# Attention scores of a two-block transformer on one core: only 512 key columns a head in the dilated layer, and latent-attention heads on halves and quarters of the rows

## What is computed

```python
A_PATTERNS = ((128, 1), (512, 4), (2048, 16))      # window, dilation
def dilated_band_attention(q, k, v, window, dilation):
    """Centred dilated window: query t attends t + j*dilation, |j| <= window/(2*dilation)."""
...
    wts = jax.nn.softmax(lses, axis=0)
    return jnp.einsum('pbsh,pbshc->bshc', wts.astype(q.dtype), outs)
```

```python
    q_c = jnp.concatenate([q_nope, q_rope], axis=-1)[:, :, :, None]
    k_c = jnp.concatenate([k_nope, jnp.broadcast_to(k_rope[:, :, None], (b, s, C_HEADS, C_ROPE))], axis=-1)
    c_out = block_attention(q_c, k_c, v_c)
```

## Time and profile before

| | us |
|---|---|
| median of 3 runs | 4381.66 |
| lowest, highest | 4380.32, 4391.59 |
| the profiled execution | 4382.55 |
| its span on the core | 4380.8 |

### The profile page before, as it was taken

How to read it: one execution, slowest core, us unless ns; L and a number is a source line. 1 busy time by engine, 2 the same in 40 slices (tenths; PEclk the granted TensorE clock), 3 DMA queues, 4 the chain that set the end, 5 groups by cost and what they waited for, 6 DMA issues and landing times. The chain is left out here.

```text
span 4380.8 us, 56560 instructions
## 1 busy us (share of the span) xinstructions
PE 3830.7 (87%) x22320; PEld 3130.2 (71%) x22320; DVE 2545.0 (58%) x3879; ACT 1673.6 (38%) x2291; POOL 334.7 (8%) x207
## 2 busy tenths in 40 slices
PE   6988999988989999998898999499678898994996
PEld 2666778767777888887796877277577786872774
DVE  6256772159765566556334763677654566735775
ACT  2223332146330000003114763267534565732775
POOL 0001111000000000000000000033100000000441
PEclk9989999989999999999999999699889999996998
DMA  7101123230432111112213004299723203032997
GB/s 288 59 23 56 58 73 97 82 132 20 154 135 82 38 57 38 57 39 86 89 58 143 31 16 151 87 370 364 247 65 105 53 21 114 14 137 80 367 376 277
DMA packets 178217, 518.88 MB, mean 118 GB/s; under 512 B 20000, under 2 KB 113344, under 8 KB 159952
## 3 DMA queue, kind: packets, MB, share of 16 engines
q1 hardware_dynamic: 158384, 454.42, 28.6%
q0 software_dynamic: 16496, 59.36, 4.6%
q10 hardware_dynamic: 3120, 2.10, 0.2%
HBM read 427.21 MB, written 88.62 MB: 118 GB/s over the span
## 5 line engine op out<-in xcount | busy, mean ns | idle before, releaser
L2077 ACT ACTIVATE mlp_relu<-mlp_z 128x512 f32<-128x512 f32 x64 | 38.3, 598 | 616.0 <-PE mlp_z L157 616.0
L3174 DVE TENSOR_TENSOR ring_r<-ring,oN_r 128x4096 fp32r<-128x4096 f32 x48 | 212.1, 4423 | 70.0 <-ACT oN_r L3105 69.9
L155 PE MATMUL scans_G<-ring_r 128*128 128x512 f32 x544 | 221.7, 408 | 32.3 <-ACT scans_stg L2624 18.3
L3174 DVE TENSOR_TENSOR ring_r<-ring,hT_r 128x4096 fp32r<-128x4096 f32 x48 | 212.4, 4424 | 55.4 <-ACT hT_r L3105 55.3
L3105 ACT ACTIVATE oN_r<-ring 128x4096 fp32r<-128x4096 f32 x48 | 174.0, 3630 | 86.7 <-DMA ring<-in_w_all 73.4
L155 PE MATMUL mlp_z<-oN_r,mlp_w_high_r 128*128 128x512 f32 x512 | 200.2, 391 | 5.6 <-DVE ring_r L2118 5.6
L3105 ACT ACTIVATE hT_r<-ring 128x4096 fp32r<-128x4096 f32 x48 | 174.0, 3630 | 68.2 <-DMA ring<-in_w_all 68.0
L156 PE MATMUL mlp_z<-hT_r,mlp_w_high_r 128*128 128x512 f32 x512 | 199.9, 390 | 0.0
L157 PE MATMUL mlp_z<-oN_r,ring_r 128*128 128x512 f32 x512 | 199.9, 390 | 0.0
L155 PE MATMUL mlp_y_ps<-mlp_w_high_r,ring_r 128*128 128x512 f32 x512 | 199.6, 390 | 0.0
L157 PE MATMUL mlp_y_ps<-mlp_w_high_r,ring_r 128*128 128x512 f32 x512 | 199.2, 389 | 0.0
(11 more groups left out here) (644 smaller groups left out, 10515.0 us busy)
## 6 DMA issues: line engine op xcount, KB each, us to landing
ring<-in_w_all SPq DMA_DIRECT2D x118, 2048.0 KB, 10.6
ring<-in_w_mlp SPq DMA_DIRECT2D x16, 2048.0 KB, 7.7
ring<-in_w_all SPq DMA_DIRECT2D x12, 1024.0 KB, 6.3
branch_gates<-scans_stg SPq DMA_DIRECT2D x48, 256.0 KB, 2.0
merge_raw<-branch_gates SPq DMA_DIRECT2D x16, 768.0 KB, 5.1
ring<-in_w_even SPq DMA_DIRECT2D x4, 1536.0 KB, 6.7
qk_turned<-even_gemm_y SPq DMA_DIRECT2D x48, 128.0 KB, 1.9
even_qk<-qk_turned SPq DMA_DIRECT2D x6, 1024.0 KB, 4.9
```

The costliest lines, as they stand in the source:

```text
L155: pe.matmul(out, lh, rh, start=start, stop=False)
L2077: act.activation(r[:, n % 2, :], Z[:, n % 4, :], ACT.Relu).then_inc(z_free, 1)
L3174: dve.tensor_tensor(buf_r[:, b, :], buf[:, b, :], w_high[n % RING].bitcast(F32), ALU.subtract)\
```

## The change

**Even attention** gets a stage of its own, `even_stage`. A block scores 512 columns a head in place of 1024: 256 keys around the block (its 128 tokens and 64 on either side) in three passes on F32R, and for each of the four classes modulo 4 the 32 queries of the class against the 256 keys of that class, as eight plain float32 matmuls (4 classes by 2 heads; 64 rows, 32 stationary columns, 256 moving columns read with a step of 4 elements), each writing 32 partitions. For this the queries of a block are kept in the order of their classes. The shift, the exponential, the transposes (8 a block) and the copies into `pT` halve. The values are made with `pT` stationary: for each head 2 matmuls with the near values (128 stationary, 64 moving columns) and 8 with the class values (32 stationary, 64 moving columns). The result is scaled on DVE (`norm`), turned once on PE (`turn_out`) and copied by ACT into `hT` in token order (`take_out`). q, k and their high parts lie in two ring slots, so this stage feeds two weight slots, and the other two are fed by the out_even stage behind its x loads. The values come in five DMAs a pair in place of one (1.2 MB in place of 0.5), and the table in eight.

**Latent attention**: the 64 position-free components of the two heads go on rows 0 to 63 and 64 to 127, as in even and gqa. The rotary 32 come as a second set: for each pass four matmuls on rows 0, 32, 64 and 96 onwards (2 heads by 2 halves of the keys), added to the same banks. `mla_gemm` writes ten tiles of 128 rows and one of 32, by 5 transposes a step (6 in every other), two ACT copies where three were, no copy of the shared part, one DMA a step and a small second one in every other. `w_mla` is laid out for this by twelve DMAs in place of one.

```diff
-            sp.dma_start(w_mla.rearrange("p (h n) -> p h n", h=8), m["w_mla"].rearrange("h p n -> p h n")).then_inc(mla_in, 16)
+            for g in range(2):
+                heads = m["w_mla"][4 * g:4 * g + 4, :, :].rearrange("h p n -> p h n")
+                for to, of, n in ((0, 0, 64), (256, 64, 32), (384, 96, 64), (640, 160, 32), (768, 192, 64), (1024, 256, 64)):
+                    at = g * (MLA_W // 2) + to
+                    sp.dma_start(w_mla[:, at:at + 4 * n].rearrange("p (h n) -> p h n", h=4), heads[:, :, of:of + n])                      .then_inc(mla_in, 16)
...
-                    for j in range(2 * G):
-                        ins = pe.transpose(TP[0:W, i % 2, j, :], x[:, i % 3, j * W:(j + 1) * W], m["ident"][:])
-                    ins.then_inc(xt_done, 1)
+                    if i % 2 == 0:
+                        pe.transpose(TP[0:RO, 0, NB, :], keep_rope[:, i // 2, :], m["ident"][:])
+                    for j in range(2):
+                        pe.transpose(TP[:, i % 2, j, :], x[:, i % 3, j * P:(j + 1) * P], m["ident"][:])
+                        pe.transpose(TP[:, i % 2, 2 + j, :], x[:, i % 3, KN + j * P:KN + (j + 1) * P], m["ident"][:])
+                    pe.transpose(TP[:, i % 2, 4, :], x[:, i % 3, 2 * P:KN], m["ident"][:]).then_inc(xt_done, 1)
...
-                        sp.dma_start(qk[:, b, :, a, :], m["qkT"][8 * a + 2 * p:8 * a + 2 * p + 2, 0:96, :]
-                                     .rearrange("h p n -> p h n")).then_inc(qk_in[b], 16)
+                        sp.dma_start(qk[:, b, a * S:(a + 1) * S], m["qkT"][5 * g + 2 * a + j, :, :]).then_inc(qk_in[b], 16)
+                    for hd in range(2):
+                        for half in range(2):
+                            r = 64 * hd + 32 * half
+                            sp.dma_start(qk[r:r + 32, b, QR], m["qkT"][5 * g + 4, 64 * j + 32 * hd:64 * j + 32 * hd + 32, :])\
+                              .then_inc(qk_in[b], 16)
+                            if p == 0:
+                                sp.dma_start(qk[r:r + 32, 0, KR], m["qkT"][10, 0:32, half * HALF:(half + 1) * HALF])\
...
-                        for hd in range(2):
-                            for half in range(2):
-                                cols = slice(half * HALF, (half + 1) * HALF)
-                                ins = three_passes(pe, SA[:, 2 * hd + half, :],
-                                                   [q_[:, b, hd, 0, toks] for q_ in (qk_high, qk_low)],
-                                                   [k_[:, b, hd, 1, cols] for k_ in (qk_high, qk_low)], True, True)
-                            ins.then_inc(scored, 1)
+                        (qh, kh), (ql, kl) = ((t_[:, b, 0:S][:, toks], t_[:, b, S:2 * S]) for t_ in (qk_high, qk_low))
...
+                    passes = ((qh, kh), (qh, kl), (ql, kh))
+                    for half in range(2):
+                        cols = slice(half * HALF, (half + 1) * HALF)
+                        for j, (q_, k_) in enumerate(passes):
+                            for hd in range(2):
+                                r = slice(64 * hd, 64 * hd + 64)
+                                ins = pe.matmul(SA[:, 2 * hd + half, :], q_[r, :], k_[r, cols], start=j == 0,
+                                                stop=j == 2 and not mla)
+                                if half == 1 and j == 2 and not mla:
+                                    ins.then_inc(scored, 1)
+                    if mla:
+                        (qh, kh), (ql, kl) = ((t_[:, b, QR][:, toks], t_[:, 0, KR]) for t_ in (qk_high, qk_low))
+                        for j, (q_, k_) in enumerate(((qh, kh), (qh, kl), (ql, kh))):
+                            for hd in range(2):
+                                for half in range(2):
+                                    r = slice(64 * hd + 32 * half, 64 * hd + 32 * half + 32)
+                                    ins = pe.matmul(SA[:, 2 * hd + half, :], q_[r, :], k_[r, :], start=False, stop=j == 2)
+                                if j == 2:
+                                    ins.then_inc(scored, 1)
...
+def even_stage(nc, m):
+
+
+    with Stage(nc, "even") as st:
+        PAIRS, NEAR, CLS = 6, 2 * P, 4
+        N, SUB, WIN = PAIRS * NT, P // CLS, 384
+        LEN = S // CLS
+        SCALE = 0.125
+        spare = [(m["ring"].used + 2 + j) % RING for j in range(2)]
...
+                b = p % 2
+                if p >= 2:
+                    sp.wait_ge(scored, 2 * NT * (p - 1))
+                sp.dma_start(raw[:, b, :, :], m["qkT"][2 * p:2 * p + 2, :, :].rearrange("a p n -> p a n")).then_inc(qk_in[b], 16)
+                if p == 0:
+                    rows = m["dilated"].rearrange("(i r) n -> r i n", r=CLS)
+                    for r in range(CLS):
+                        sp.dma_start(table[SUB * r:SUB * r + SUB, 0:WIN], rows[r, :, 896 - P:896 - P + WIN]).then_inc(near_in, 16)
+                    for r in range(CLS):
+                        sp.dma_start(wide_table[SUB * r:SUB * r + SUB, :], rows[0, :, :]).then_inc(wide_in, 16)
+                if p >= 2:
+                    sp.wait_ge(pv_done, NT * (p - 1))
+                v = m["v"][:, P * p:P * p + P]
+                for tiles, first in ((slice(0, 7), 64), (slice(7, 9), 0), (slice(9, 11), S - NEAR)):
+                    count = (tiles.stop - tiles.start) * P
+                    sp.dma_start(v_near[:, b, tiles, :], v[first:first + count, :].rearrange("(t p) c -> p t c", p=P))\
+                      .then_inc(v_in[b], 16)
+                for half in range(2):
...
+            def scores(n):
+                p, qb = divmod(n, NT)
+                b, toks = p % 2, slice(qb * P, (qb + 1) * P)
+                if qb == 0:
+                    pe.wait_ge(low, 2 * (p + 1))
+                if n >= 2:
+                    pe.wait_ge(shifted, 2 * (n - 1))
+                for r in range(CLS):
+                    for hd in range(2):
+                        d = slice(64 * hd, 64 * hd + 64)
+                        pe.matmul(SA[SUB * r:SUB * r + SUB, 2 * (n % 2) + hd, NEAR:HALF], raw[d, b, 0, toks][:, r::CLS],
+                                  raw[d, b, 1, r::CLS], start=True, stop=True)
+                keys = slice(first_key(qb), first_key(qb) + NEAR)
+                (qh, kh), (ql, kl) = ((t_[:, b, 0, toks], t_[:, b, 1, keys]) for t_ in (qk_high, qk_low))
+                for j, (q_, k_) in enumerate(((qh, kh), (qh, kl), (ql, kh))):
+                    for hd in range(2):
+                        d = slice(64 * hd, 64 * hd + 64)
+                        ins = pe.matmul(SA[:, 2 * (n % 2) + hd, 0:NEAR], q_[d, :], k_[d, :], start=j == 0, stop=j == 2)
+                        if j == 2:
...
+            def turn(u):
...
+                for k in range(4):
...
+            def values(w):
+                p, qb = divmod(w, NT)
+                b = p % 2
+                if qb == 0:
+                    pe.wait_ge(v_in[b], 16 * 5 * (p // 2 + 1))
+                if w >= 2:
+                    pe.wait_ge(taken, w - 1)
+                for hd in range(2):
+                    pe.wait_ge((ev_act, ev_dve)[hd], w + 1)
+                    pt, c = pT[:, (2 * w + hd) % 4, :, :], slice(64 * hd, 64 * hd + 64)
+                    for k, t in enumerate(near_tiles(qb)):
+                        pe.matmul(O[:, w % 2, c], pt[:, k, :], v_near[:, b, t, c], start=k == 0, stop=False)
+                    for half in range(2):
+                        for r in range(CLS):
+                            i = slice(SUB * r, SUB * r + SUB)
+                            ins = pe.matmul(O[i, w % 2, c], pt[:, 2 + half, i], v_class[:, b, half, r, c], start=False,
...
+            def turn_out(w):
+                pe.wait_ge(normed, w + 1)
+                pe.transpose(OT[:, w % 2, :], o[:, w % 2, :], m["ident"][:]).then_inc(o_turned, 1)
+
+            for n in range(-1, N + 2):
+                if n + 1 < N:
+                    scores(n + 1)
+                if 0 <= n < N:
+                    turn(2 * n)
+                if n >= 2:
+                    turn_out(n - 2)
+                if 1 <= n <= N:
+                    values(n - 1)
+                if 0 <= n < N:
+                    turn(2 * n + 1)
+
...
+                act.activation(m["hT"][:, p, qb * P:(qb + 1) * P].rearrange("p (i r) -> p r i", r=CLS),
+                               OT[:, w % 2, :].rearrange("p (r i) -> p r i", r=CLS), ACT.Copy).then_inc(taken, 1)
+
...
+                    dve.wait_ge(t_done, u - 3)
+                dve.memset(wait_taker[:, u % 4:u % 4 + 1], 0.0)
+                dve.tensor_tensor_reduce(out=sc[:, u % 4, :].rearrange("p (w c) -> p w c", w=2),
+                                         in0=SA[:, u % 4, :].rearrange("p (w c) -> p w c", w=2),
+                                         in1=times_of(u // 2 % NT), scale=-SCALE, scalar=-LOWEST, op0=ALU.add, op1=ALU.min,
+                                         accum_out=nm[:, u % 8:u % 8 + 1]).then_inc(shifted, 1)
...
```

(10 more changed lines are left out.)

234 lines of the change are left out of this document (172 added, 62 removed).

## The result

The changed kernel takes 4316.0 us (4 runs, 4308.2 to 4318.9), the kernel before, run beside it, 4383.7. The ratio is **0.984, with a 95% interval of 0.982 to 0.985**: 65 to 77 us gained. 4327 had been predicted, in a range of 4288 to 4372.

A forecast was written before the change was run, and what follows sets the result against it. PE was taken to bound both attentions. Gains of 39.8 us (even blocks), 3, 5, 5.1, 2.4 and 1, less 1.5 lost, sum to 54.8: from 4382.55 to 4327.7, 4327 as a median, range 4288 to 4372.

The forecast's parts named there:

- Even block: Even attention, one block on PE: parts sum to 4.81 us against 5.64, 39.8 us gained in 48 blocks.
- class scores: Even block on PE: eight two-pass matmuls, all eight side by side at about 0.06 each, 0.50 us.
- class values: Even block on PE: 16 matmuls at 0.06 each, 0.96 us.
- seven changes: Even block on PE: seven changes of tile shape at 0.16 each, 1.12 us.
- the stepped read: Rival, even class scores: reading keys with a 16-byte step halves the stream; 0.95 us, 21.6 us more, 4349; chance 0.13.
- 16 x 0.06, the issue rate again: Even class values: 16 matmuls priced by how fast matmuls can be issued, 0.96 us; small transposes started some 0.07 apart.
- all side by side: Rival, even and mla blocks: no issue bound; class values 0.3, rotary 0.69, even block 4.1 to 4.2; 4295 us; chance 0.14.
- The two slow rivals: Even and mla blocks: only two tiles work side by side, 4424 us, chance 0.10; or each matmul costs 0.109, 4402, 0.08.
- Pair changes: Even stage: DVE's low part and ACT's casts no longer fit in one block; 0.3 for each of five, 1.5 us lost.
- Start: Even stage's first loads and cast: smaller loads ahead, and two half casts let DVE start before ACT ends; 3 us gained.
- mla_gemm, 5 predicted: mla_gemm's 16 steps: both sides of the balance shorten by about 0.3 us a step, 5 us gained, ends 3 and 6.
- Latent attention, 6.50 predicted: mla block on PE: 6.50 us against 6.66, rotary part 0.72 by issue; 5.1 us gained, pair changes 2.4 more.

The follow-up runs named there:

- the two experiments: Changed kernel with, per mla_gemm step, one more 128-column copy on DVE (2.55 us a step) or two more transposes on PE (2.57), against 2.41.
- class_order: Changed kernel with even_gemm writing q and k with each 128 tokens sorted by class: 4289.2 us, 0.977 of the kernel before.

## Why the prediction was right, and where its terms were not

The mechanism was right: PE bounds both attentions before and after, and small tiles run side by side. The forecast was 11 us too high, and inside it larger errors stood against each other. By the stretches 17 us more were gained than the sum has, and stages outside the change hide 8 of them in the span. So that the time came out this close is in part luck.

- **Even block, 4.81 predicted, 4.62 measured.** Term by term, with 0.14 for a change of shape (predicted, then measured):

| term | predicted | measured |
|---|---|---|
| class scores | 0.50 | 0.93 (1.07 less a change) |
| near scores | 0.37 | 0.35 (three of 0.117) |
| transposes, turn_out | 0.98 | 0.98 |
| near values | 0.88 | 0.89 |
| class values | 0.96 | 0.45 (0.36 less a change, twice) |
| seven changes | 1.12 | 1.0 (what is left of 4.62) |

  Two terms failed, in opposite directions. (The near scores' 0.37 was a slip: three times half of 0.23 is 0.35.) *Class scores*: the stepped read, which the prediction held as a rival with 0.95 and a chance of 0.13, is real. *Class values*: the step "16 x 0.06, the issue rate again" was wrong. It took the 0.07 of four small transposes as a bound on how fast matmuls can be issued; passes start 7 ns apart here, and sixteen take 0.22 us. The rival that priced this about rightly (all side by side, 0.3) gave 4295 since it had no stepped read beside it. The two rivals were treated as exclusive; both came true, and that they cancelled to 0.08 us is luck.
- **The Trainium skill on tiles** (TensorE: Matmul & The Clock Gate, Part 3) was followed only halfway in the prediction, which kept its own bound from a row against "starts about 4 ns apart". The trace agrees with the page's rule: in the rotary part four F32R matmuls start 3 to 4 ns apart, as the page has it. Passes on plain float32 start 6 to 7 ns apart.
- **The Trainium skill on the step** (SBUF — State Buffer, Specifications: 16-byte cachelines, with a penalty for each cross to a new line) is borne out in the direction. It names no size. Here a pass of 256 keys goes from 0.24 to 0.44 us when the keys step by 16 bytes in place of lying in runs of 32 (queries in a row in both), and from 0.27 to 0.47 against keys in one row (queries stepped in both).
- **The two slow rivals** (two tiles at a time, 0.109 a matmul) are out by the same rows: eight tiles start within 0.047 us.
- **Pair changes, 1.5 us lost predicted, 2.1 gained.** "Before, it fitted" was wrong: the kernel before has a block of 6.06 in place of 5.64 at each of five pair changes, which one block of the earlier trace rows didn't show. In the changed kernel the casts (3.1 us) and DVE's low part (3.3) are even longer than assumed, and are hidden all the same. They begin to show in blocks of 4.33 and cost 0.4 us a pair change at 4.15 and 0.8 at 3.85; of the 0.8 the larger part stands behind ACT's cast.
- **Start, 3 predicted, 0.5 measured, and a term that was missing, 6.2.** The two half casts are not equal. ACT and DVE, with q first and k behind it, where the earlier trace rows had one cast of 1.91 for 2048 columns:

```profile
2344.33 2.02 ACT L1453 ACTIVATE ring_r<-ring 128x1024 fp32r<-128x1024 f32 x1 [9.44 <-DMA ring<-qk_turned]
2346.25 1.04 ACT L1455 ACTIVATE ring_r<-ring 128x1024 fp32r<-128x1024 f32 x1
2346.38 2.00 DVE L1494 TENSOR_TENSOR even_qk_low<-ring,ring_r 128x1024 fp32r<-128x1024 f32 x1 [12.46 <-ACT ring_r L1453]
2348.29 1.22 DVE L1498 TENSOR_TENSOR even_qk_low<-ring,ring_r 128x1024 fp32r<-128x1024 f32 x1
```

  q, read with the step, takes 2.0 on both, k half of that or little more. The load brought 1.3 us (from the first load to the first cast 7.9 before, 6.6 now; 5.8 to 7.1 over the traces) and cast and low part took 0.9 of it back (4.4 to the first scores before, 5.2 now). But from the first scores to the first values it is 8.0 us in place of 14.2: the fill of the pipeline, which the sum had left out, halves with the work of a block, and the second block's scores no longer wait for a shift of the first.
- **Sum of the even stage:** blocks 47.8 in place of 39.8, pair changes +3.6 beside the forecast, fill +6.2, start -2.5, the last blocks +0.6: 57.2 in place of 41.3.
- **mla_gemm, 5 predicted and 5.0 measured**, for the reason given as far as the two experiments reach; what the fewer DMAs and the shorter copies gave wasn't told apart. `w_mla` in twelve pieces cost nothing that can be seen: `odd_gemm` to the start of mla_gemm is 154.6 us before and 155.1 after.
- **Latent attention, 6.50 predicted and 6.54 measured**: the rotary part at 0.76 without its change, close to 0.72, but the reason for the 0.72, twelve matmuls by issue, was wrong here too. Its four tiles start within 0.01 us, and the next four 0.23 us later (0.34 the first time): it is the other price in the prediction, three rounds side by side. Blocks gave 4 us where 5.1 were predicted, pair changes 4.3 where 2.4 were (a pair change costs 0.6 over a block now, and cost 2.0).
- No wait for the weight slots that are fed later is seen: out_even takes 116.0 us after and 116.3 before, and in the MoE stage behind it the third weight cast, of one of those slots, starts 22.3 us behind the stage's first work after and 22.9 before. The stage as a whole takes 406.5 and 402.7 us. With one trace of the kernel before, and 401 to 409 in those that feed so, a cost of a few us isn't excluded.

## What to carry to other kernels

Price tiles of an array by how many run side by side, then look at the operands' strides: a small layout change in the stage that writes them brought 21 us more in the even stage (455.8 to 435.1 with even_gemm), and added no instruction. Where a sum has both an unproved speed and an unproved slowness, weigh them together, since both can be true. And count what lies at the ends: the fill of a pipeline shrinks with its block, and a stall at every eighth block is only seen in a row of eight.

## What the runs showed of the hardware

- Eight float32 matmuls on 64x32 tiles start within 47 ns of each other, and then their eight second passes follow together. From start to start that is 6 to 7 ns, and 3 to 4 for F32R matmuls on four 32x128 tiles.
- Each of four column tiles of 32 takes a pass of 64 moving columns every 56 ns, though a weight load alone takes some 0.11 us; on all 128 columns such a pass costs 0.111.
- Reading SBUF with a step of 16 bytes takes 1.6 to 1.9 times as long on three engines: PE 0.24 to 0.44 a pass (256 columns), ACT 1.04 to 2.02 and DVE 1.22 to 2.00 (1024 columns each). A step of 128 bytes costs ACT and DVE the same (2.03 and 1.98 in `class_order`). Runs of 32 elements cost PE about nothing. ACT's read of PSUM with a step of 16 bytes costs nothing (0.379 with and without).
- Going between matmuls on 128 and on 32 columns costs 0.14 us a change. Behind a change to the near or the rotary scores, 0.11 us more lies between the first matmuls and the next on the same tiles (0.223 in place of 0.117, 0.337 in place of 0.23).
